# Memory attention's output products taken one head at a time: new turns for xq and xo, weight splits in other units, one product tile held back in the first `down`

## The reference, cut to what matters

```python
def memory_cross_attention(xn, memn, w_q, w_kv, w_o):
    q = (xn @ w_q).reshape(B, S, XA_HEADS, XA_HEAD_DIM)      # 4 heads of 256
    ...
    s = jnp.einsum("bshd,bmhd->bhsm", q, k) * XA_HEAD_DIM ** -0.5
    o = jnp.einsum("bhsm,bmhd->bshd", jax.nn.softmax(s, axis=-1), v)
    return o.reshape(B, S, D).astype(xn.dtype) @ w_o

def conv_ffn(xn, w_up, w_conv, w_down):
    u = causal_depthwise_conv(xn @ w_up, w_conv)
    a, g = jnp.split(u, 2, axis=-1)
    return (a * jax.nn.silu(g)) @ w_down
```

## Time and profile before

| | |
|---|---|
| median of 3 runs | 1410.81 us (1410.29 to 1410.99) |
| profiled execution | 1409.39 us, its span 1407.6 us |
| mean granted TensorE clock | 0.997 of full |
| TensorE busy | 1390.0 us, 99% |
| VectorE busy | 842.6 us, 60% |
| ScalarE busy | 556.5 us, 40% |
| DMA | 144.01 MB, mean 102 GB/s |

### The profile page before, as it was taken

The page is one execution under the profiler, slowest core; times in us unless marked ns, Lnnn a source line. Parts: engine busy times, 40 slices in busy tenths (PEclk is TensorE's granted clock), DMA queues, the critical chain, the costliest instruction groups (busy, mean ns, idle before and its releaser), DMA issues.

```text
span 1407.6 us, 17484 instructions
## 1 busy us (share of the span) xinstructions
PE 1390.0 (99%) x6510; PEld 1122.1 (80%) x6510; DVE 842.6 (60%) x1151; ACT 556.5 (40%) x760; POOL 115.8 (8%) x136
## 2 busy tenths in 40 slices
PE   9999999999999999999999999999999999999997
PEld 7777785688878878888888888877888888888886
DVE  7757785344456765764676676767775444434445
ACT  6545684233344532332334554533333222212231
POOL 1010155000000000000000221023000000000000
PEclk9999999999999999999999999999999999999999
DMA  7232346221122233222321223331123232322221
GB/s 263 81 105 82 114 151 224 105 91 61 40 81 90 89 120 117 93 90 90 110 99 64 116 90 106 119 135 47 73 90 120 100 110 99 110 90 90 92 88 60
DMA packets 28022, 144.01 MB, mean 102 GB/s; under 512 B 3146, under 2 KB 8547, under 8 KB 13368
## 3 DMA queue, kind: packets, MB, share of 16 engines
q1 hardware_dynamic: 24616, 133.71, 26.8%
q0 software_dynamic: 2656, 8.72, 1.9%
q10 hardware_dynamic: 688, 0.73, 0.2%
HBM read 136.84 MB, written 6.30 MB: 102 GB/s over the span
## 4 chain that ended last, share of the span: by engine, by line
PE 93%; DVE 3%; ACT 2%; issue 1%; DMA 0%; SPq 0%; DVEq 0%; ACTq 0%
PE ps L1839 27%; PE ps L1841 27%; PE ps L1840 27%; PE ps L2208 2%; PE ps L2264 1%; PE ps L2062 1%; PE ps L2251 1%; ACT w_hi L627 1%; PE ps L2053 1%; PE ps L2075 1%; DVE w_lo L1114 1%; PE ps L2383 0%; PE ps L2385 0%; PE ps L2389 0%; PE ps L2101 0%
## 5 line engine op out<-in xcount | busy, mean ns | idle before, releaser
L1839 PE MATMUL ps<-opA_hi,w_hi 128*128 128x512 f32 x1120 | 443.0, 396 | 1.1 <-DVE opA_lo L1163 0.5
L1841 PE MATMUL ps<-opA_hi,w_lo 128*128 128x512 f32 x1120 | 436.3, 390 | 0.0
L1840 PE MATMUL ps<-opA_lo,w_hi 128*128 128x512 f32 x1120 | 436.0, 389 | 0.0
L627 ACT CAST w_hi<-raw 128x2048 fp32r<-128x2048 f32 x111 | 211.6, 1907 | 284.5 <-PE ps L1841 284.4
L1114 DVE TENSOR_TENSOR w_lo<-raw,w_hi 128x2048 fp32r<-128x2048 f32 x112 | 256.8, 2293 | 106.6 <-ACT w_hi L627 104.8
L1839 PEld LDWEIGHTS ps<-opA_hi,w_hi 128*128 128x128 f32 x1120 | 210.4, 188 | 47.2 <-issue 2.8
L1841 PEld LDWEIGHTS ps<-opA_hi,w_lo 128*128 128x128 f32 x1120 | 210.2, 188 | 44.5
L1840 PEld LDWEIGHTS ps<-opA_lo,w_hi 128*128 128x128 f32 x1120 | 210.4, 188 | 44.0 <-issue 1.7
L1839 PE MATMUL ps<-opB_hi,w_hi 128*128 128x512 f32 (+1 forms) x584 | 228.9, 392 | 5.4 <-DVE opB_lo L1150 4.9
L1840 PE MATMUL ps<-opB_lo,w_hi 128*128 128x512 f32 (+1 forms) x584 | 226.3, 388 | 0.0
L1841 PE MATMUL ps<-opB_hi,w_lo 128*128 128x512 f32 (+1 forms) x584 | 226.2, 387 | 0.0
(11 more groups left out here) (376 smaller groups left out, 1414.1 us busy)
## 6 DMA issues: line engine op xcount, KB each, us to landing
raw<-weights_dram SPq DMA_DIRECT2D x113, 1024.0 KB, 4.8
g_dram<-g_stage POOLq DMA_DIRECT2D x8, 512.0 KB, 2.9
h<-x_t_dram SPq DMA_DIRECT2D x7, 512.0 KB, 5.9
g_spec<-g_dram SPq DMA_DIRECT2D x5, 512.0 KB, 3.7
scores<-g_dram SPq DMA_DIRECT2D x3, 512.0 KB, 4.8
out_dram<-h SPq DMA_DIRECT2D x6, 256.0 KB, 2.3
mem_raw<-mem_t_dram POOLq DMA_DIRECT2D x1, 1024.0 KB, 8.3
c_keys<-c_dram POOLq DMA_DIRECT2D x4, 256.0 KB, 4.0
```

What stands on the lines that cost most here:

```text
L627: A.copy(w_hi[:, p, :], raw[:, p, :]).then_inc(hi_ready, 1)
L1839: W.matmul(out, w[0], x[0], start=start, stop=False, skip_group_check=mixed)
L1840: W.matmul(out, w[0], x[1], start=False, stop=False, skip_group_check=mixed)
L1841: return W.matmul(out, w[1], x[0], start=False, stop=stop, skip_group_check=mixed)
```

## The change

Half 8 of xq runs before the first scores, so that the halves fill turns 0 to 6. xo begins in turn 7 instead of turn 10, with one tile or a few a turn, and `xo_part` waits on the low parts of no more heads than its last tile belongs to. `xo_part(2, 4, 6)` stands between the turns and the last parts. ScalarE's halves of the second xo pair and VectorE's `evac_xq(3)` move a turn ahead; VectorE's quarters go two a turn, ahead of the low part. The short `down` of the first feed-forward layer holds back one tile instead of two. Lines of the changed kernel are shifted by -3 on TensorE and +1 on VectorE.

```diff
--- before.py
+++ after.py
@@ -334,10 +334,11 @@
 
 
 
-        XQ_TURNS = {0: 8, 1: 9, 2: 10, 3: 11, 4: 12, 5: 13, 7: 14, 8: 15}
-        XO_TURNS = {10: ((0, 0, 3),), 11: ((0, 3, 4), (1, 0, 2)), 12: ((1, 2, 4),), 13: ((2, 0, 3),),
-                    14: ((0, 4, 6),), 15: ((1, 4, 6),), 16: ((2, 3, 4), (3, 0, 1)), 17: ((3, 1, 4),)}
-        XO_ENDS = ((0, 6, 8), (1, 6, 8), (2, 4, 8), (3, 4, 8))
+        XQ_TURNS = {u: 9 + u for u in range(7)}
+        XO_TURNS = {7: ((0, 0, 1),), 8: ((0, 1, 2),), 9: ((1, 0, 1),), 10: ((1, 1, 2),), 11: ((2, 0, 2), (0, 2, 3)),
+                    12: ((3, 0, 2), (0, 3, 4)), 13: ((1, 2, 4), (2, 2, 3)), 14: ((2, 3, 4), (3, 2, 3)),
+                    15: ((3, 3, 4), (0, 4, 5)), 16: ((0, 5, 6), (1, 4, 5)), 17: ((1, 5, 6),)}
+        XO_ENDS = ((0, 6, 8), (1, 6, 8), (2, 6, 8), (3, 4, 8))
 
         def unit_scores(u):
 
@@ -924,8 +925,8 @@
                     act.wait_ge(pv_done, 32 + v + 1)
                     A.copy(op_hi[1][:, 2 * (v // 4):2 * (v // 4) + 2, (v % 4) * P:(v % 4 + 1) * P],
                            ps[:, 7, 0:M].rearrange("p (a t) -> p a t", a=2)).then_inc(pv_hi, 1)
-                if u in (3, 4, 8, 9):
-                    g, part = FIRST["xo"] + u // 8, (u - 3) % 5
+                if u in (3, 4, 7, 8):
+                    g, part = FIRST["xo"] + u // 7, (u - 3) % 4
                     cols = slice(part * CHUNK, (part + 1) * CHUNK)
                     if part == 0:
                         act.wait_ge(raw_in[g % 2], 16 * (g // 2) + 16)
@@ -1575,21 +1576,17 @@
                     lowest(u + 1)
                 if u < 16:
                     normalise(32 + u, u)
+                if u in (4, 5, 9, 10):
+                    for n in range(2):
+                        split_quarter(FIRST["xo"] + u // 8, 2 * (u in (5, 10)) + n)
                 if u >= 2:
                     v = u - 2
                     dve.wait_ge(pv_hi, 4 + v + 1)
                     lo_part(op_lo[1][:, 2 * (v // 4):2 * (v // 4) + 2, (v % 4) * P:(v % 4 + 1) * P],
                             ps[:, 7, 0:M].rearrange("p (a t) -> p a t", a=2),
                             op_hi[1][:, 2 * (v // 4):2 * (v // 4) + 2, (v % 4) * P:(v % 4 + 1) * P]).then_inc(pv_lo, 1)
-                if u in (3, 8):
-                    evac_xq(2 + u // 8)
-                if 5 <= u < 8:
-                    split_quarter(FIRST["xo"], u - 5)
-                if u == 7:
-                    split_quarter(FIRST["xo"], 3)
-                if u in (10, 11):
-                    split_quarter(FIRST["xo"] + 1, 2 * u - 20)
-                    split_quarter(FIRST["xo"] + 1, 2 * u - 19)
+                if u in (3, 7):
+                    evac_xq(2 + u // 7)
             tail("xo", "g_ffn", 0, 2, 2)
             norm(3)
             V.memset(z_pad[:, :, :, 0:2], 0.0)
@@ -2273,12 +2270,11 @@
                     if c % 2 == 0:
                         pair_ready(g)
                     pe.wait_ge(bank_read, 2 * FIRST["xo"] + c - 3)
-                    pe.wait_ge(pv_lo, 12)
-                elif first == 4 and end == 6:
-                    pe.wait_ge(pv_lo, 16)
+
+                pe.wait_ge(pv_lo, 8 + 4 * ((end - 1) // 2))
                 return chunk(g % 2, c % 2, X[1], ps[:, c, :], range(first, end))
 
-            for n in (0, 2, 1, 3, 4, 5, 6, 7):
+            for n in (0, 2, 1, 3, 4, 5, 6, 7, 8):
                 xq_half(n)
             x_qk(0)
             x_qk(1)
@@ -2293,7 +2289,7 @@
                     transpose_unit(32 + u - 1, 2)
                 if u >= 2:
                     x_pv(u - 2)
-            pe.wait_ge(pv_lo, 20)
+            xo_part(2, 4, 6)
             for turn in XO_ENDS:
                 xo_part(*turn).then_inc(chunk_done, 1)
             gemm("xo", X[1], begun=True)
@@ -2301,7 +2297,7 @@
 
             for n, g in enumerate(FFN_ORDER):
                 gemm(f"up1_{g}", X[0], operand=None if n else next_lo, count=16, norms=() if n else [(0, 2)])
-                gemm(f"down1_{g}", X[1], n_k=FFN_GROUPS[g], operand=act_lo, count=FFN_COUNT[g], wide=3, late=2 if n < 2 else 1)
+                gemm(f"down1_{g}", X[1], n_k=FFN_GROUPS[g], operand=act_lo, count=FFN_COUNT[g], wide=3, late=2 if n == 1 else 1)
 
 
             gemm("hy_in", X[0], operand=next_lo, count=24, norms=[(0, 3)], pairs=8)
```

## The result

The changed kernel takes 1403.53 us (median of 5 runs, 1403.40 to 1403.90); the kernel before took 1410.81 beside it (5 runs, 1410.10 to 1411.16). The ratio is 0.9949, with a 95% interval of 0.9936 to 0.9963. The forecast was 1404.3 with a range of 1402.0 to 1407.4. The profiled execution took 1403.40, with a span of 1401.6 where 1401.1 was forecast.

The account below looks back on a forecast made before the run. TensorE, busy 1390.0 of 1407.6 us, bounds the kernel, so only its waits can shorten it. Savings of 8.80 less 2.28 added give 6.5 us net: 1404.3 from the 1410.81 median, range 1402.0 to 1407.4.

Parts of the forecast that it names:

- The stage: From the norm's first product ahead of memory attention to the short down's first product; prediction's terms there give 5.29 us less.
- Turn 9: Memory attention: wait for unit 7's values before xo's first product goes, 2.23 us, plus 1.56 at low clock; together 3.79.
- Turn 0: Memory attention: with half 8 ahead of the first scores, the wait before unit 2's scores goes, saving 1.00 us.
- Turn 14, the end and bare turns: Waits before turn 14 and the last products go, 1.15 us each, 2.30; filling bare turns 6 and 9 saves 0.48.
- Short `down`: First short down: 45 products instead of 39 ahead of its last tile remove its wait, 1.23 us, margin 0.13.
- Turn 11: New wait of TensorE for the second half of xo's splits on VectorE: 0.7 us, bounds 0.4 and 1.2.
- Turn 17: New wait before unit 15's values, only three products standing after unit 14's values: 0.36 us.
- chunk 4: New wait for chunk 4's split weights, the last block covering with 30 products instead of 36: 1.0 us.
- Rival 1: No new waits of note, VectorE keeping pace in turns 8 to 10: 8.6 us less, 1402.2; chance 0.10.
- Rival 2: Turn 11's wait lowers the clock again, or turns 8 to 10 show several waits: 1406.7 us; chance 0.18.
- Rival 3: Waits only move; VectorE and ScalarE need 3.5 us a turn in turns 8 to 11: 1410.6; chance 0.08.
- Rival 4: Slower: clock drops to 1.2 GHz through three-product turns 7 to 10, net +4.3 us, 1415.1; chance 0.04.

Follow-up runs that it names:

- two_tiles_turn10: Kernel before with turn 10's xo block cut from three tiles to two and xo waiting only for heads it reads: median 1406.81 us, ratio 0.998.
- before_again: The kernel before, unedited, run and profiled a second time: median 1409.18 us, ratio 0.9996 to the same program under its own name.
- late_only: Kernel before with only the short down's edit, its last tile alone held back (late=1): median 1408.46 us, ratio 0.9988.
- half_8_first: Kernel before with only half 8 of xq ahead of the first scores, later halves moved up, turn 8 without products: median 1409.61 us, ratio 0.9997.
- after_twice: The changed kernel, unedited, run again on one chip beside a repeat of the all_three kernel: median 1404.19 us, ratio to before 0.9961.
- all_three: Changed kernel with xo's products reordered against its three new waits (turn 11, turn 17, chunk 4) at once: median 1401.38 us, ratio to before 0.9938.
- turn17_six: Changed kernel with six products in turn 17 and the turns from 13 on rearranged: median 1403.13 us, ratio to before 0.9957.
- ends_36: Changed kernel with 36 products instead of 30 in the last block, turns 12 and 13 holding six: median 1403.21 us, ratio to before 0.9951.
- turn11_swapped: Changed kernel with chunk 0's products ahead of chunk 2's in turn 11: median 1403.32 us, ratio to before 0.9955.
- all_three_twice: The all_three kernel run again, on another chip: median 1401.32 us, ratio to before 0.994.
- old_split_place: Changed kernel with xo's second pair's splits back in their old turns and chunk 2's products one turn later: median 1405.10 us, ratio 0.997.

## Why the prediction was right

- **The stage.** Forecast 5.29 us less, measured 5.32. Chunk 4's first product comes at 405.85, 89.64 after the norm's; before it stood at 410.79 (410.8 in the prediction, worked out; the row is below), 95.11 after it. That is 5.47 earlier, and 5.3 was forecast. The span came out 0.5 above the forecast because this execution began its stage 0.53 later.

```profile
410.79 0.39 PE L1839 MATMUL ps<-opB_hi,w_hi 128*128 128x512 f32 x1
```

- **Turn 9, 3.79.** Shown, in both its parts: 2.16 for the wait (two_tiles_turn10 against before_again; 2.23 forecast), 1.57 for the clock (before against before_again; 1.56). But the prediction took the low clock as a sure cost of the wait. It was there in two of the four traces that have this wait (before and late_only, not before_again and half_8_first). As a mean it is worth less than 1.56, and the gain of 5.6 in the session of after_twice fits with that.
- **Turn 0, 1.00.** The wait is gone, but the term isn't one of that edit: alone it brings nothing (half_8_first). The prediction listed it and the filled turns as separate terms. The sum is right since the change makes both; the split between them is not settled by a measurement of its own.
- **Turn 14, the end and bare turns, 2.30 and 0.48.** No experiment took these alone. No wait stands at turn 15 or before the last products, and if turn 0 brought its 1.00, the sum of the stage leaves 0.1 to 0.3 us for an error in them; errors that cancel would not be seen.
- **Short `down`, 1.23.** Shown: 1.2 to 1.5 by the stretch from there to the end over all traces, and the span's 6.0 less the stage's 5.32, plus 0.53 of later start, leaves 1.2.
- **Turn 11, 0.7.** Measured 0.59, and 0.56 by taking it away. The chain on VectorE came as worked out: values of unit 5 at 365.36, the last two quarters done 9.4 later (9.4 to 9.5 forecast), the first of its rows being the evacuations and the last the quarters:

```profile
367.20 1.28 DVE L1134 SCALAR_TENSOR_TENSOR xq<-ps,rstd 128x512 f32<-128x512 f32 x2
368.39 0.41 DVE L1569 TENSOR_REDUCE low<-ps 128x1 f32<-128x256 f32 x1
...
369.98 0.42 DVE L1151 TENSOR_TENSOR opB_lo<-ps,opB_hi 128x256 fp32r<-128x256 f32 x1 [0.71 <-ACT opB_hi L926]
...
371.11 1.29 DVE L1563 TENSOR_TENSOR w_lo<-raw,w_hi 128x512 fp32r<-128x512 f32 x2
...
373.44 1.29 DVE L1563 TENSOR_TENSOR w_lo<-raw,w_hi 128x512 fp32r<-128x512 f32 x2
```

- **Turn 17, 0.36, and chunk 4, 1.0.** Measured 0.47 and 0.98; taking them away gave 0.59 and 1.14. Both were there for the reason given, the number of products between two dependent steps. Turn 17 was taken too small because the step between two units' values came out at 2.07 (393.62 to 395.69), not 1.97.
- **The rivals.** Rival 1 (no new waits) falls by the three waits; a version without them exists all the same, all_three, and it lies 2.3 us lower in the stage. Rival 2 (a wait of turn 11 that lowers the clock) falls by the 0.59 and the clock of 1.00. Rival 3 asked for 3.5 us a turn on VectorE; the turns took 2.67. Rival 4 asked for product steps of 0.43 in turns 7 to 10; the turns step by 2.67 at a clock of 1.00. The Trainium skill, page "TensorE: Matmul & The Clock Gate", section "A second HAM failure mode: psum-queue depth-cycling", describes small idles between groups of matmuls, in a kernel that cycles through PSUM banks, that keep the clock changing. This trace has short groups and no such effect; turns 7 to 10 have no idle time between them, so the rule isn't contradicted.
- **The product step.** The 216 ns that the prediction quotes from the Trainium skill, same page, section "Back-to-back issue gap", is there the gap of a single matmul in isolation, not of a stream. The 0.2266 read over 38 products decides here, and the wait of chunk 4 came out at 0.98, not at the 1.3 worked out from the page's figure.
- **The range.** The bounds that the prediction names, 0.4 and 1.2 for the wait of turn 11 and 0.6 for rounding, give 1403.4 to 1405.4, not 1403.2 to 1405.5. The measured 1403.53 lies in both.
- **The median.** 1404.3 was made from 1410.81 less 6.5. Measured is 7.3 less in the first session and 5.6 in the last. Two things that differ from one execution to the next can make such a difference: whether the clock fell after the wait of turn 9, and the program's start. The mechanism was right; that the trace of before happened to be one with the fall is luck. Against before_again the stage is 3.75 shorter, not 5.32, and with that trace in hand the same working would have had no term for the clock.

What stays open: why the clock falls after the same 1.99 us of idle in one execution and not in another, and why the load of `f_out` makes TensorE wait for 0 to 1.99 us near 193 us.

## What to carry to other kernels

Count from each dependent step how many independent products stand behind it, and compare with what its result takes to come back: here 1.97 us for the values of a unit, and 7.8 us for a whole-pair split, so six products (turn17_six) and 36 products (ends_36) hide them, three and 30 don't. Put ready work first inside a turn (turn11_swapped) and keep a filler in each turn; a wait that is taken away where work is merely moved forward comes back where the work is now missing (half_8_first). For differences below 1 us compare stages between two landmarks of the traces, since medians of whole runs move by more than that from one session to the next.

## What the runs showed of the hardware

- After TensorE had been idle for 1.96 to 1.99 us behind turn 9, the granted clock was 0.54 over the next 3.7 us, that is mostly 1.2 GHz, in two traces (before, late_only), and 1.00 in two others (before_again, half_8_first). It was also 1.00 behind the 1.99 us of idle at 195.18 in all_three_twice. So the length of the idle time alone does not decide. After shorter idle times, up to the 1.43 us of old_split_place, it stayed at 1.00 in the stretches read. When it falls it costs 1.57 us, about a quarter of the 6.0 us that the span became shorter.
- The same instructions ahead of 316 us took up to 2.7 us longer in one trace than in another, most of it in one wait for a load (0 to 1.99 us of idle near 193 us).
- Four turns of 2.67 us, each with three products of 128x512 between small matmuls, ran at a granted clock of 1.00 throughout.
